# ScalarE's order of block transfers and exponentials in the state-space stages of a hybrid decoder step

## The chip, the cores and the metric

The kernel runs on one core of one Trainium2 chip. A core has five engines that run their own instruction streams and meet at semaphores: PE (TensorE, matmuls and transposes), DVE (VectorE), ACT (ScalarE), POOL (GpSimd) and SP (SyncE, which here only issues transfers). ACT issues transfers too; they stand in its stream between its computations, so a transfer that waits for a semaphore holds back everything behind it on ACT. The metric is the device time of one execution in microseconds (us), lower is better.

## The reference

One step of a two-layer decoder: an attention layer (left as it is here) and a Mamba-2 layer, over a prompt of 16 + 512 tokens and 8 samples of 4 tokens. The part that matters is the state-space part of the Mamba-2 layer:

```python
def ssd_chunked(x, dt, A, B, C, init_state, chunk):
    a_cum = jnp.cumsum(dtg * A.reshape(g, e).astype(f32), axis=2)
    xdt = xg * dtg[..., None]
    seg = a_cum[:, :, :, None] - a_cum[:, :, None, :]
    decay = jnp.exp(jnp.where(causal, seg, -jnp.inf))
    cb = jnp.einsum('bcign,bcjgn->bcijg', Cg, Bg)
    y_diag = jnp.einsum('bcijg,bcijge,bcjgep->bcigep', cb, decay, xdt)
    decay_to_end = jnp.exp(a_cum[:, :, -1:] - a_cum)
    chunk_states = jnp.einsum('bcjgn,bcjge,bcjgep->bcgepn', Bg, decay_to_end, xdt)
    ...
    y_off = jnp.einsum('bcign,bcgepn,bcige->bcigep', Cg, starts, jnp.exp(a_cum))
    y = (y_diag + y_off).reshape(b, L, h, p)
```

`decay` is a 128 x 128 matrix for each head and each chunk, and `exp(a_cum)` a row of 128 for each head and chunk. The states run from chunk to chunk.

## The kernel before

Projections are done in fp32 as three matmuls of a high and a low part (`project`, L1202 to L1204); a weight slab of 1 MB is loaded by SP into one of two buffers, ACT writes its high part (`split_hi`, L689) and POOL the low part (`split_lo`, L608, four instructions). Four attention stages come first, then four state-space stages, one for each group g of 8 heads. PE weaves projections of the stage and the next one between the steps of the state-space part.

A group has six units u: u = 0 is the 32 sample tokens, u = 1 the 16 meta tokens, u = 2 to 5 the four chunks of 128 tokens (called blocks here). The steps of block u, and where they stand:

- `load_a(g, u)` (L985, issued by ACT): the block's cumulative logs are copied out of a scratch in DRAM to all 128 partitions of a tile `seg`, 0.5 MB. There are three such tiles: blocks 2, 3, 4, 5 take tiles 1, 2, 0, 1. Tile 2 lies where the sample states 6 and 7 are held, so `load_a(g, 3)` waits until SP's stores of those two (`out<-s_in`, L564) have landed (`sn_out[6]`, `sn_out[7]`). `load_a(g, 4)` waits for unit 0's matmuls, `load_a(g, 5)` for block 2's (`b_done`).
- POOL subtracts the block's own logs (L660, once the transfer has landed), then ACT clamps and exponentiates the tile (`decays`, L1057 and L1059), then DVE multiplies by the scores (`mix`, L2003).
- `load_ec(g, u)` (L997, ACT, two transfers): the rows for `exp(a_cum)`; blocks 4 and 5 use the two tiles `ec` again, after DVE's `add_skip` of block 2 or 3 (`d_done`). `start_decay(u)` (L1063, ACT) exponentiates them; `add_skip(u)` (L2037 to L2040, DVE) uses them.
- PE: `part_a` (scores and transposes of the block), then `part_b` (L1521 needs `mix`; L1531; L1535 ends with `b_done`).
- POOL's `decay_state` (L621) scales the running state after `b_done`, DVE's `new_state` (L2017) adds to it.

The order on each engine is written out by hand, and no scheduler changes it. PE runs `part_a(u)`, `part_b(u-1)`, one projection, and so on. POOL runs, for blocks 3 to 5, the subtraction of block u, then `decay_state(u-1)`; in the last group POOL splits the last two weight slabs ahead of block 3's subtraction. DVE runs `prepare(u)`, `new_state(u-1)`, `mix(u)`, a projection's evacuation, `add_skip(u-1)`. In the last group the very last slab's high part goes to a tile of its own (`w_hi_last`). At the end of a group ACT squares the gated output (`square_y`, L1122), which PE sums (`sum_y`, L1542).

Of the kernel before, what the change touches and what calls it, by code (L numbers as in the profile page):

```python
# [44 lines left out]
UNITS = len(ORDER)  # L45
# [76 lines left out]
def z_order(stage):  # L122

    if stage == STAGES - 1:
        return [(t, half) for half in range(2) for t in range(4)]
    return [(t, half) for t in range(4) for half in range(2)]
# [37 lines left out]
def build(nc, x_prompt, x_sample, cache_k, cache_v, state_conv, state_ssm, meta_tokens, norm_w,  # L164
# [14 lines left out]
    def slab_done(n):  # L179
        kind, stage, i = slabs[n]  # L180
        return tile_done(kind, stage, per_slab[kind] * (i + 1) - 1)
# [36 lines left out]
    with ctx:  # L218
# [207 lines left out]
        def seg_no(u):  # L426

            return u - 1 if u else 0
# [15 lines left out]
        def high_buf(n):  # L444

            return w_hi_last if n + 1 == len(slabs) else w_hi_buf[n % HI_SLOTS]
# [222 lines left out]
        def _(act):  # L669
# [9 lines left out]
            def split_hi(count=1):  # L679
                for _ in range(count):  # L680
                    n = done[0]
                    m = slab_elems[slabs[n][0]]
                    act.wait_ge(w_raw[n % RAW_SLOTS], raw_target[n])
                    if n + 1 == len(slabs):
                        for b in range(4):
                            act.wait_ge(sn_out[b], 16 * GROUPS)
                    elif n >= HI_SLOTS:
                        act.wait_ge(p_done, slab_done(n - HI_SLOTS))
                    act.activation(high_buf(n)[:, 0:m], raw[n % RAW_SLOTS][:, 0:m],  # L689
                                   ACT.Copy).then_inc(w_hi, 1)  # L690
                    done[0] += 1

            def exp_tables():
                act.preload_act_table_set("natural_log_exp_and_others")
# [276 lines left out]
            def load_a(g, u):  # L971

                c, i = ORDER[u], seg_no(u)
                n = LEN[c]
                if i == 0 and g:
                    act.wait_ge(b_done, UNITS * g)
                if i == 1:
                    act.wait_ge(cn_out, 96 * (g + 1))
                if i == 2:
                    for b in (6, 7):  # L980
                        act.wait_ge(sn_out[b], 16 * (g + 1))
                if i >= 3:
                    act.wait_ge(b_done, UNITS * g + (3 if i == 4 else 1))
                src = a_scratch[SSM_H * g:SSM_H * (g + 1), COL[c]:COL[c] + n]
                act.dma_start(seg[i % SEG_SLOTS][0:n, :, 0:n],  # L985
                              src.partition_broadcast(n)).then_inc(e_in[i % SEG_SLOTS], 16)

            def load_ec(g, u):

                c = ORDER[u]  # L990
                if u >= 4:
                    act.wait_ge(d_done, 5 * g + u - 2)
                elif g:
                    act.wait_ge(d_done, 5 * (g - 1) + u + 2)
                src = a_scratch[SSM_H * g:SSM_H * (g + 1), COL[c]:COL[c] + P].rearrange("(t e) n -> e t n", e=2)
                for i in range(2):
                    act.dma_start(ec[u % 2][64 * i:64 * i + 64, :, :],  # L997
                                  src[i].partition_broadcast(64)).then_inc(ec_in[u % 2], 16)
# [7 lines left out]
            for g in range(GROUPS):  # L1006
# [44 lines left out]
                def decays(u):  # L1051
                    w = 5 * g + seg_no(u)
                    n = LEN[ORDER[u]]
                    act.wait_ge(seg_done, w + 1)
                    e = seg[seg_no(u) % SEG_SLOTS][0:n, :, 0:n]

                    act.activation(e, e, ACT.Relu, scale=-1.0).then_inc(clamped, 1)  # L1057
                    act.wait_ge(clamped, w + 1)
                    act.activation(e, e, ACT.Exp, scale=-1.0).then_inc(l_done, 1)  # L1059

                def start_decay(u):
                    act.wait_ge(ec_in[u % 2], 32 * (2 * g + (u - 2) // 2 + 1))
                    act.activation(ec[u % 2][:, :, :], ec[u % 2][:, :, :], ACT.Exp).then_inc(ec_ready, 1)  # L1063
# [26 lines left out]
                def silu_z(parts):  # L1090
                    for t, half in parts:
                        act.wait_ge(p_evac, half_no[("z", s, t, half)] + 1)
                        act.activation(z[:, t, span("z", s, half)], z[:, t, span("z", s, half)],
                                       ACT.Silu).then_inc(silu_ready, 1)

                for u in range(2, UNITS):
                    decays(u)
                    if u == 2:
                        if g + 1 == GROUPS:
                            split_hi()  # L1100
                        load_a(g, 3)
                        load_a(g, 4)
                    if u == 3:
                        load_a(g, 5)
                        if g + 1 < GROUPS:
                            split_hi()
                    start_decay(u)
                    if 4 <= u + 1 < UNITS:
                        load_ec(g, u + 1)
                    if (g, u) == (GROUPS - 1, 2):  # L1110
                        silu_z(z_order(s)[0:HEADS])
                        exp_tables()
# [556 lines left out]
        def _(dve):  # L1669
# [40 lines left out]
            def soft_max(s, u):  # L1710

                c, v = ORDER[u], UNITS * s + u
                n, cc, b = rows_of(c), colsum(c), v % 2
                dve.wait_ge(s_done, v + 1)
                dve.wait_ge(c_ready, 2 * s + (2 if u else 1))
                if v >= 2:
                    dve.wait_ge(t_done, v - 1)
                if c == 5:
                    dve.tensor_tensor_reduce(sm[b][:, 0:1024], fS, cst[:, C_SATT:C_SATT + 1024], 1.0, 2 * NEG,
                                             ALU.add, ALU.max, mx[:, b, 0:1])  # L1720
                    link(dve.tensor_tensor_reduce(sm[b][:, 1024:1056], misc[:, 32:64],
                                                  cst[:, C_SATT + 1024:C_SATT + 1056], 1.0, 2 * NEG,
                                                  ALU.add, ALU.max, mx[:, b, 1:2]))
                    w = 1
                    link(dve.tensor_tensor(mx[:, b, 0:1], mx[:, b, 0:1], mx[:, b, 1:2], ALU.max))
                    sink = sink_rows[:, s:s + 1]
                else:
                    _, nk, m0 = keys_of(c)
                    for h in range(HEADS):
                        ins = dve.tensor_tensor_reduce(sm[b][0:n, h * 256:h * 256 + nk], fS[0:n, h * 256:h * 256 + nk],  # L1730
                                                       cst[0:n, C_MASK + m0:C_MASK + m0 + nk], 1.0, 2 * NEG,
                                                       ALU.add, ALU.max, mx[0:n, b, h:h + 1])
                    link(ins)
                    w = 4
                    sink = sinks[0:n, 4 * s:4 * s + 4]
                link(dve.tensor_tensor(mxc[0:n, 0:w], mx[0:n, b, 0:w], crow[0:n, cc:cc + w], ALU.mult))
                link(dve.tensor_tensor(msk[0:n, 0:w], mxc[0:n, 0:w], sink, ALU.max))
                dve.tensor_scalar(nm[0:n, b, 0:w], msk[0:n, 0:w], -1.0, None, ALU.mult)
                dve.tensor_tensor(ds[0:n, b, 0:w], sink, msk[0:n, 0:w], ALU.subtract).then_inc(soft_a, 1)
# [487 lines left out]
```

## Time and profile before

| | us |
|---|---|
| median of 3 runs (lowest, highest) | 1024.51 (1024.32, 1026.81) |
| the profiled execution, its own time | 1027.62 |
| span of its trace | 1024.7 |
| PE busy | 980.9 (96%) |
| DVE, ACT, POOL busy | 581.2, 466.9, 365.8 |
| share of PE in the chain that ended last | 79% |

In the rows further down, a timeline row gives the start in the span, the duration, the engine, the line of the kernel, the operation, the tile written and those read, and in square brackets how long the engine had been idle and what ended that. "issue" means that the profile shows no wait that ended there. A waits row gives the waiting instruction, whom it waited for, the sum, how often, and the longest. In a row by stretch the columns are the length, then the busy time of PE, PE's weight loads, DVE, ACT and POOL with their counts, the granted clock of PE, the DMA engines' share and GB/s. Times are us from the start of the span. Group g = 0 of the state-space part has its blocks at 575 to 615, the next two repeat it about 124 and 248 later, and the last (g = 3) has them at 945 to 987.

### The profile page before, as it was taken

How to read it: one execution, taken by the hardware profiler on the slowest of the kernel's cores; microseconds unless marked ns; L12 is line 12 of the kernel's file. 1: busy time of each engine (PE TensorE's matmuls, PEld its weight loads, DVE VectorE, ACT ScalarE, POOL GpSimd, SP SyncE). 2: the span in 40 equal slices, each digit the busy share in tenths (PEclk: the TensorE clock that was granted, in tenths of full speed). 3: DMA queues.
4: the chain of work that ended last, by engine and by line, in shares of the span. 5: the costliest groups of instructions: out<-in, count | busy, mean ns of one | idle time of the engine just before them, and what ended most of it. 6: DMA issues, size and time to landing. Idle time of an engine off the chain costs nothing.

```text
span 1024.7 us, 18539 instructions
## 1 busy us (share of the span) xinstructions
PE 980.9 (96%) x7372; PEld 902.1 (88%) x7372; DVE 581.2 (57%) x1433; ACT 466.9 (46%) x819; POOL 365.8 (36%) x275
## 2 busy tenths in 40 slices
PE   8999999999999999999997999999999999999988
PEld 7988899989998899978986889998799978997867
DVE  5114431354224431356685787966889577986772
ACT  5324623365134623366444364343552445526453
POOL 4240233113330233115533335534354244443610
PEclk9999999999999999999998999999999999999999
DMA  6351221242233222101423715247242563416303
GB/s 198 101 155 62 83 83 53 85 157 65 66 103 141 84 83 59 73 21 42 148 86 87 226 44 157 83 111 205 62 136 84 148 186 82 137 47 207 92 11 98
DMA packets 144117, 106.35 MB, mean 104 GB/s; under 512 B 10258, under 2 KB 135364, under 8 KB 143840
## 3 DMA queue, kind: packets, MB, share of 16 engines
q1 hardware_dynamic: 115032, 92.24, 29.0%
q10 hardware_dynamic: 29000, 12.94, 4.8%
q8 instruction: 58, 0.95, 0.4%
q14 instruction: 27, 0.22, 0.1%
HBM read 92.44 MB, written 16.79 MB: 107 GB/s over the span
## 4 chain that ended last, share of the span: by engine, by line
PE 79%; DVE 10%; issue 4%; DMA 3%; ACT 2%; POOL 2%; ACTq 0%; SPq 0%; DVEq 0%; POOLq 0%
PE pp L1202 19%; PE pp L1204 19%; PE pp L1203 18%; PE pS L1318 3%; DMA w_raw_buf<-in_w_attn_in 2%; PE pS L1542 2%; DVE cv L1914 2%; PE pO L1364 1%; PE pO L1363 1%; PE pO L1535 1%; PE pO L1531 1%; PE pT_ L1521 1%; PE pO L1482 1%; POOL w_lo_raw L608 1%; DVE z L2056 1%
## 5 line engine op out<-in xcount | busy, mean ns | idle before, releaser
L608 POOL TENSOR_TENSOR w_lo_buf<-w_raw_buf,w_hi_buf 128x512 fp32r<-128x512 f32 x214 | 288.0, 1377 | 503.0 <-ACT w_hi_buf L689 272.0
L1202 PE MATMUL pp<-h_hi,w_hi_buf 128*128 128x280 f32 (+1 forms) x1248 | 379.6, 304 | 7.8 <-POOL w_lo_buf L608 2.9
L1204 PE MATMUL pp<-h_hi,w_lo_buf 128*128 128x280 f32 (+1 forms) x1248 | 364.1, 292 | 0.0
L1203 PE MATMUL pp<-h_lo,w_hi_buf 128*128 128x280 f32 (+1 forms) x1248 | 363.5, 291 | 0.0
L1202 PEld LDWEIGHTS pp<-h_hi,w_hi_buf 128*128 128x128 f32 x1248 | 236.7, 190 | 19.0 <-issue 11.7
L1203 PEld LDWEIGHTS pp<-h_lo,w_hi_buf 128*128 128x128 f32 x1248 | 236.4, 189 | 4.6 <-issue 4.1
L1204 PEld LDWEIGHTS pp<-h_hi,w_lo_buf 128*128 128x128 f32 x1248 | 236.4, 189 | 0.0
L689 ACT ACTIVATE w_hi_buf<-w_raw_buf 128x2048 fp32r<-128x2048 f32 (+1 forms) x55 | 104.1, 1892 | 38.7 <-DMA w_raw_buf<-in_w_ssm_in 16.9
L1700 DVE TENSOR_TENSOR x<-x,pp 128x272 f32<-128x272 f32 (+3 forms) x128 | 56.4, 440 | 80.3 <-PE pp L1204 79.4
L1202 PE MATMUL pp<-og_hi,w_hi_buf 128*128 128x280 f32 (+2 forms) x256 | 76.2, 298 | 1.8 <-DVE og_lo L1821 1.1
L1204 PE MATMUL pp<-og_hi,w_lo_buf 128*128 128x280 f32 (+2 forms) x256 | 75.2, 294 | 0.0
L1203 PE MATMUL pp<-og_lo,w_hi_buf 128*128 128x280 f32 (+2 forms) x256 | 75.1, 293 | 0.0
L1914 DVE SCALAR_TENSOR_TENSOR cv<-rb,par,cv 128x584 f32<-128x584 f32 x69 | 69.1, 1001 | 1.1
L1202 PE MATMUL pp<-y_hi,w_hi_buf 128*128 128x272 f32 (+2 forms) x224 | 66.5, 297 | 1.8 <-DVE x L1700 1.5
L1203 PE MATMUL pp<-y_lo,w_hi_buf 128*128 128x272 f32 (+2 forms) x224 | 64.5, 288 | 0.0
L1694 DVE TENSOR_TENSOR q<-pp,rs 128x280 f32<-128x280 f32 x32 | 14.4, 450 | 82.4 <-PE pp L1204 82.4
L1057 ACT ACTIVATE seg<-seg 128x1024 f32<-128x1024 f32 (+1 forms) x20 | 18.6, 932 | 83.5 <-issue 48.4
L1204 PE MATMUL pp<-y_hi,w_lo_buf 128*128 128x272 f32 x192 | 55.4, 289 | 0.0
L1202 PEld LDWEIGHTS pp<-og_hi,w_hi_buf 128*128 128x128 f32 x256 | 48.8, 191 | 2.9 <-issue 2.6
L1773 DVE TENSOR_TENSOR gate<-pp,rs 128x280 f32<-128x280 f32 x32 | 14.4, 449 | 63.8 <-PE pp L1204 63.8
L1203 PEld LDWEIGHTS pp<-og_lo,w_hi_buf 128*128 128x128 f32 x256 | 48.9, 191 | 0.2 <-issue 0.2
L1204 PEld LDWEIGHTS pp<-og_hi,w_lo_buf 128*128 128x128 f32 x256 | 48.8, 191 | 0.0
(334 smaller groups left out, 1730.0 us busy)
## 6 DMA issues: line engine op xcount, KB each, us to landing
w_raw_buf<-in_w_attn_in SPq DMA_DIRECT2D x16, 1024.0 KB, 5.2
w_raw_buf<-in_w_ssm_in SPq DMA_DIRECT2D x16, 1024.0 KB, 5.4
w_raw_buf<-in_w_attn_out SPq DMA_DIRECT2D x8, 1024.0 KB, 5.1
s_in<-in_state_ssm SPq DMA_DIRECT2D x32, 256.0 KB, 4.2
out<-s_in SPq DMA_DIRECT2D x32, 256.0 KB, 3.0
seg<-a_scratch ACTq DMA_DIRECT2D x16, 512.0 KB, 4.1
w_raw_buf<-in_w_ssm_out SPq DMA_DIRECT2D x8, 1024.0 KB, 5.6
w_raw_buf<-in_w_attn_in SPq DMA_DIRECT2D x8, 512.0 KB, 5.9
```

What stands on the lines that cost most here:

```text
L608: ins = pool.tensor_tensor(low_buf(n)[:, piece], raw[n % RAW_SLOTS][:, piece], high_buf(n)[:, piece].bitcast(F32), ALU.subtract)
L689: act.activation(high_buf(n)[:, 0:m], raw[n % RAW_SLOTS][:, 0:m], ACT.Copy).then_inc(w_hi, 1)
L1057: act.activation(e, e, ACT.Relu, scale=-1.0).then_inc(clamped, 1)
L1202: pe.matmul(dst, hi[:, k, cols], a_hi[:, k, tk], start=(k == 0), stop=False)
L1203: pe.matmul(dst, hi[:, k, cols], a_lo[:, k, tk], start=False, stop=False)
L1204: mm = pe.matmul(dst, lo[:, k, cols], a_hi[:, k, tk], start=False, stop=(k == depth - 1))
L1318: mm = pe.matmul(fS[0:n, h * 256:h * 256 + nk], q[:, h, COL[c]:COL[c] + n], kq[:, k0:k0 + nk], start=True, stop=True)
L1542: mm = pe.matmul(pS[:, part, 0:tk.stop - tk.start], ones[:, :], xc[:, t, tk], start=(t == 0), stop=(t == HEADS - 1))
L1694: dve.tensor_tensor(dst[:, tk], bank(kind, s, tile, half), rs[:, tk], ALU.mult).then_inc(p_evac, 1)
L1700: dve.tensor_tensor(x[:, tile, tk], x[:, tile, tk], bank("out", s, tile, half), ALU.add).then_inc(p_evac, 1)
L1773: dve.tensor_tensor(gate[:, t, tk], bank("gate", s, t, half), rs[:, tk], ALU.mult).then_inc(p_evac, 1)
L1914: ins = dve.scalar_tensor_tensor(w[:, 0:CONV_OUT], r[:, tap:tap + CONV_OUT], conv_wc(tap, ct), w[:, 0:CONV_OUT], ALU.mult, ALU.add)
```

## The change

Two moves in ACT's stream, in every group. The transfers of blocks 4 and 3 (in this order now) are issued ahead of block 2's `decays`, where they stood behind it in the other order. And `load_ec` of blocks 4 and 5 is issued behind that block's own `decays`, where it stood one block earlier, behind `start_decay` of the block before. Nothing is added or taken out, and the streams of the other engines are the same.

```diff
                 for u in range(2, UNITS):
+                    if u == 2:
+                        load_a(g, 4)
+                        load_a(g, 3)
                     decays(u)
                     if u == 2:
                         if g + 1 == GROUPS:
                             split_hi()
-                        load_a(g, 3)
-                        load_a(g, 4)
                     if u == 3:
                         load_a(g, 5)
                         if g + 1 < GROUPS:
                             split_hi()
+                    if u >= 4:
+                        load_ec(g, u)
                     start_decay(u)
-                    if 4 <= u + 1 < UNITS:
-                        load_ec(g, u + 1)
```

ACT's stream in group 0, at block 2 (`seg1` is block 2's tile, `seg2` block 3's, `seg0` block 4's; the same in groups 1 and 2):

```order
 L1089 ACTIVATE sT1_138<-pT_ 128x512 [waits yo_done]
-L1057 ACTIVATE seg1_119<-seg1_119 128x1024 [waits seg_done]
-L1059 ACTIVATE seg1_119<-seg1_119 128x1024 [waits clamped]
+L985 DMA seg0_118<-a_scratch 128x8x128 [waits b_done]
 L985 DMA seg2_120<-a_scratch 128x8x128 [waits sn_out7,sn_out6]
-L985 DMA seg0_118<-a_scratch 128x8x128 [waits b_done]
+L1057 ACTIVATE seg1_119<-seg1_119 128x1024 [waits seg_done]
+L1059 ACTIVATE seg1_119<-seg1_119 128x1024 [waits clamped]
 L1063 ACTIVATE ec0_126<-ec0_126 128x512 [waits ec_in0]
```

Both transfers now stand ahead of block 2's two activations, and the activations stand behind a wait for two stores.

ACT's stream in the last group, at the same place (`w_hi_last` is the last weight slab's high part, which POOL's last split reads):

```order
 L1089 ACTIVATE sT1_138<-pT_ 128x512 [waits yo_done]
+L985 DMA seg0_118<-a_scratch 128x8x128 [waits b_done]
+L985 DMA seg2_120<-a_scratch 128x8x128 [waits sn_out7,sn_out6]
 L1057 ACTIVATE seg1_119<-seg1_119 128x1024 [waits seg_done]
 L1059 ACTIVATE seg1_119<-seg1_119 128x1024 [waits clamped]
 L689 ACTIVATE w_hi_last_134<-w_raw0_buf_54 128x2048 [waits sn_out2,sn_out1,sn_out3,sn_out0,w_raw0]
-L985 DMA seg2_120<-a_scratch 128x8x128 [waits sn_out7,sn_out6]
-L985 DMA seg0_118<-a_scratch 128x8x128 [waits b_done]
 L1063 ACTIVATE ec0_126<-ec0_126 128x512 [waits ec_in0]
```

Here the two transfers also pass the last slab's high part.

ACT's stream at block 4, before (`ec0` holds block 4's rows):

```order
L1063 ACTIVATE ec1_127<-ec1_127 128x512 [waits ec_in1]
L997 DMA ec0_126<-a_scratch 64x4x128 [waits d_done]
L997 DMA ec0_126<-a_scratch 64x4x128
L1057 ACTIVATE seg0_118<-seg0_118 128x1024 [waits seg_done]
L1059 ACTIVATE seg0_118<-seg0_118 128x1024 [waits clamped]
L1063 ACTIVATE ec0_126<-ec0_126 128x512 [waits ec_in0]
```

and now:

```order
L1063 ACTIVATE ec1_127<-ec1_127 128x512 [waits ec_in1]
L1057 ACTIVATE seg0_118<-seg0_118 128x1024 [waits seg_done]
L1059 ACTIVATE seg0_118<-seg0_118 128x1024 [waits clamped]
L997 DMA ec0_126<-a_scratch 64x4x128 [waits d_done]
L997 DMA ec0_126<-a_scratch 64x4x128
L1063 ACTIVATE ec0_126<-ec0_126 128x512 [waits ec_in0]
```

Block 4's activations no longer stand behind the wait for DVE's `add_skip`; block 5 is the same with `seg1` and `ec1`.

## Rows read from the trace of the kernel before

**Rows 1.** Page, first line.

```profile
span 1024.7 us, 18539 instructions
```

**Rows 2.** Waits of PE, 570 to 612 (us in total, times, longest).

```profile
PE pT_ L1521 <- issue: 2.1, 3, 1.0
```

**Rows 3.** Waits of PE, 942 to 982.

```profile
PE pS L1542 <- ACT xc L1122: 4.0, 1, 4.0
```

**Rows 4.** Timeline of PE, 570 to 625 (start, duration, instruction, [idle before it]).

```profile
586.90 1.09 PE L1521 MATMUL pT_<-seg,xdt 128*64 128x128 f32 x16 [0.42 <-issue]
...
588.92 1.02 PE L1535 MATMUL pO<-xw,btok 128*128 128x512 f32 x2
...
594.67 1.09 PE L1521 MATMUL pT_<-seg,xdt 128*64 128x128 f32 x16 [0.95 <-issue]
...
602.33 1.09 PE L1521 MATMUL pT_<-seg,xdt 128*64 128x128 f32 x16 [0.77 <-issue]
```

**Rows 5.** Timeline of POOL, 570 to 612.

```profile
588.35 2.27 POOL L660 TENSOR_TENSOR seg<-seg,tok 128x1024 f32<-128x1024 f32 x1 [5.16 <-DMA seg<-a_scratch]
590.59 1.04 POOL L621 TENSOR_TENSOR state<-state,ealast 128x512 f32<-128x512 f32 x1
591.59 1.89 POOL L660 TENSOR_TENSOR seg<-seg,tok 128x1024 f32<-128x1024 f32 x1
...
598.80 2.35 POOL L660 TENSOR_TENSOR seg<-seg,tok 128x1024 f32<-128x1024 f32 x1
```

**Rows 6.** Timeline of DVE, 570 to 612.

```profile
585.58 1.22 DVE L2003 TENSOR_TENSOR seg<-seg,cbm 128x1024 f32<-128x1024 f32 x1
...
592.85 1.72 DVE L2003 TENSOR_TENSOR seg<-seg,cbm 128x1024 f32<-128x1024 f32 x1 [0.43 <-ACT seg L1059]
...
600.66 1.57 DVE L2003 TENSOR_TENSOR seg<-seg,cbm 128x1024 f32<-128x1024 f32 x1 [0.67 <-ACT seg L1059]
```

**Rows 7.** Timeline of ACT, 560 to 610 (ACTq: its queue issues a transfer).

```profile
583.23 1.06 ACT L1057 ACTIVATE seg<-seg 128x1024 f32<-128x1024 f32 x1 [6.92 <-POOL seg L660]
...
584.38 1.02 ACTq L985 DMA_DIRECT2D seg<-a_scratch  x2
```

**Rows 8.** Timeline of SP, 573 to 577.

```profile
575.81 0.92 SPq L564 DMA_DIRECT2D out<-s_in  x2
```

**Rows 9.** Line L564, issued 576.1 to 576.6: issue to landing.

```profile
DMA to landing us min/median/max: 2.2/2.4/2.6
```

**Rows 10.** Line L985, issued 584.3 to 584.8: issue to landing.

```profile
DMA to landing us min/median/max: 3.8/3.8/3.8
```

**Rows 11.** Busy time by stretch: engines, PEclk, DMA share, GB/s last.

```profile
584.00:585.00 1.00, 1.00 (x10) 1.00 (x9) 0.97 (x3) 0.97 (x2) 0.00 (x0) 1.00 1.06 376
```

**Rows 12.** The same, 576.5 to 588.2.

```profile
576.50:588.20 11.70, 11.28 (x93) 9.98 (x91) 9.89 (x18) 2.75 (x3) 6.70 (x5) 1.00 0.96 287
```

**Rows 13.** Timeline of ACT, 928 to 1003.

```profile
945.75 1.05 ACT L1057 ACTIVATE seg<-seg 128x1024 f32<-128x1024 f32 x1
...
947.79 1.90 ACT L689 ACTIVATE w_hi_last<-w_raw_buf 128x2048 fp32r<-128x2048 f32 x1
951.71 1.01 ACTq L985 DMA_DIRECT2D seg<-a_scratch  x2
```

**Rows 14.** Timeline of POOL, 928 to 1003.

```profile
950.09 5.50 POOL L608 TENSOR_TENSOR w_lo_raw<-w_raw_buf,w_hi_last 128x512 fp32r<-128x512 f32 x4
955.63 2.29 POOL L660 TENSOR_TENSOR seg<-seg,tok 128x1024 f32<-128x1024 f32 x1
962.23 1.04 POOL L621 TENSOR_TENSOR state<-state,ealast 128x512 f32<-128x512 f32 x1 [4.31 <-PE pO L1535]
```

**Rows 15.** Timeline of DVE, 928 to 1003.

```profile
956.68 2.32 DVE L2003 TENSOR_TENSOR seg<-seg,cbm 128x1024 f32<-128x1024 f32 x1
```

**Rows 16.** Timeline of PE, 935 to 1025.

```profile
966.31 1.09 PE L1521 MATMUL pT_<-seg,xdt 128*64 128x128 f32 x16 [0.38 <-issue]
```

**Rows 17.** Chain of waits that ended last, 935 to 1025.

```profile
976.91 2.98 DMA ec<-a_scratch
```

## The prediction

> **What bounds the kernel now.** I read first the chain of waits, then who PE waits for in the state-space stages, then the timelines of all engines around those waits. PE is the bound: it fills nearly the whole span of 1024.7 [rows 1], so an edit on ACT is worth only what it takes out of PE's idle time, or adds to it. In group 0 PE waits three times before `part_b`, 2.1 in all [rows 2]: 0.42 before block 2, 0.95 before block 3, 0.77 before block 4 [rows 4]. Groups 1 and 2 repeat this. In the last group PE waits 4.0 for `square_y` [rows 3], and a chain of small steps sets the end there. So the edit can reach three times 2.1, and the last group.
>
> Two of the three waits look like ACT's: `mix` of blocks 3 and 4 started 0.43 and 0.67 after DVE had come free, released by ACT's exponential [rows 6]. But these two `mix` took 1.72 and 1.57, where block 2's took 1.22 [rows 6]. Set them beside POOL [rows 5]. Block 3's `mix` starts at 592.85, while POOL subtracts on block 4 from 591.59 to 593.48, and ends at 594.57, 1.09 behind POOL. Block 4's starts at 600.66, POOL works on block 5 from 598.80 to 601.15, and `mix` ends at 602.23, 1.08 behind POOL. The last group's block 2 is the same: from 956.68 with 2.32 [rows 15], while POOL subtracts from 955.63 to 957.92 [rows 14], ending 1.08 behind it. So a `mix` (two operands in SBUF) does not run beside a POOL subtraction: it stands until POOL's instruction is over. That decides what an earlier ACT is worth.
>
> **The change, part by part.** No instruction is added, so all of it is waits.
>
> (a) `decays` of blocks 4 and 5 no longer stand behind `d_done`. ACT then has block 4's exponentials ready as soon as POOL has subtracted. The gain is nothing: `mix(4)` follows `new_state(3)`, which waits for POOL's `decay_state(3)`, and POOL starts block 5's subtraction right behind that; `mix(4)` ends 1.08 behind it whether ACT is early or not. PE's 0.77 stays. `load_ec` keeps its own wait for `d_done`, and `start_decay` sat behind the landing already: in the last group the chain runs from the issue at 976.91 through 2.98 of transfer [rows 17], with no exponential on it. Cost 0, gain 0, bounds 0 to -0.77 per group.
>
> (b) The two block transfers move ahead of block 2's `decays`; queued behind `load_a(3)`'s wait are those `decays` and, in the last group, the last slab's `split_hi`. In groups 0 to 2 this wait is covered: ACT was idle for 6.92 until POOL's subtraction let `decays(2)` start at 583.23 [rows 7]. SP issued the two stores at 575.81 and about 576.3 [rows 8], the later landed 2.6 after its issue [rows 9], at 578.9. With 0.5 MB of `load_a(4)` now beside them I add up to 1.8 (its bytes at the 287 GB/s of [rows 12]), 580.7 at the latest. Still before 583.2, so it costs ACT nothing, with 2.5 of cover.
>
> What it gains: POOL waited 5.16 for block 3's transfer, subtracted from 588.35 to 590.62 [rows 5], and so began `decay_state(2)` at 590.59, though block 2's `b_done` came at 589.94 [rows 4]. With the transfer early, `decay_state(2)` starts at about 590.0, block 4's subtraction ends 0.55 earlier, and so does `mix(3)`, which hangs on that by the overlap above, not on ACT. PE's wait before block 3 falls from 0.95 to about 0.40. The last group shows that state already: there POOL was free, idle for 4.31 before `decay_state(2)` [rows 14], and PE waited 0.38 [rows 16]. Gain 0.55 a group, 1.65 in three.
>
> What it can lose: block 3's subtraction now falls early, and may fall onto `mix(2)`, which runs from 585.58 to 586.80 [rows 6] and for which PE already waits 0.42. Where does the transfer land? From the first store to the end of `load_a(3)`, 0.5 + 0.5 + 1.0 + 0.5 = 2.6 MB must pass (stores, `load_a(4)`, a weight slab, `load_a(3)`). At the best stretch's 376 GB/s [rows 11] that takes 7.0, at the mean of 287 [rows 12] 9.1. From about 576.5 (first store issued at 575.81, [rows 8]) it ends at 583.5 to 585.6. A transfer of 0.5 MB landed 3.8 after its issue [rows 10], of which its bytes are 1.5; I count 1.0 of the other 2.3 as behind the last byte. Landing: 584.5 to 586.6, and later if the next slab's load, which SP issues as soon as POOL has split the slab before, takes a share. `mix(2)` starts at 585.58. If the load lands behind that, `mix(2)` runs first, POOL subtracts from 586.8 to 588.7 while DVE has slack, and nothing is lost. I take this as the likelier half.
>
> (c) The last group. Here ACT was not idle. Before, it ran `decays(2)` at 945.75 and `split_hi` at 947.79, and then stood until 951.71 for the stores [rows 13]. Now it stands first: `load_a(3)` still goes out at 951.7, `decays(2)` runs from 952.1 to 954.2, `split_hi` until 956.1. `mix(2)` does not notice (it began at 956.68, [rows 15]). POOL does: its split of the last slab started at 950.09 and took 5.50 [rows 14], and now starts at 956.2, 6.1 later. Block 3's subtraction and `decay_state(2)` stand behind it, with 4.31 of slack [rows 14]. The excess is 6.1 - 4.31 = 1.8; 1.4 if the subtraction takes the 1.89 of [rows 5] instead of 2.29. If `load_a(4)` holds up the stores, up to 1.8 more: 3.6. I take 1.8. It goes from `decay_state(2)` through block 4's subtraction and `mix(3)` into PE, `d_done`, `load_ec(5)`, `square_y` and the end, with nothing on the way to absorb it.
>
> Sum: -1.65 + 1.8 = about +0.1 on the span of 1024.7. The profiled execution took 1027.62 by its own clock, 3 more than its span; the runs' median of 1024.51 lies at the span. I apply the difference to the median: 1024.6.
>
> **The rivals.**
> - *Collision, slower.* The transfer lands before 585.5, POOL takes block 3's subtraction ahead of `mix(2)`, and PE's wait before block 2 grows by 1.1 (as in [rows 15], 2.32 against 1.22) to 1.9 (the whole subtraction); I take 1.5. Against the 0.55 gained, each group loses 0.95, three lose 2.85, and with the last group's 1.8 it is +4.65: 1029.2. For it speaks the byte sum at the best rate, against it the next slab. It decides at a landing of 585.5 and, with one or two groups hit, lies between. The Trainium skill, "DMA: Bandwidth & Descriptors", section "Queues, rings and completion order", says that each DMA engine takes its queue rows in turn, packet by packet. By that `load_a(3)` would get its turns beside SP's weight slabs, which makes this rival likelier; no row here shows a small load in the middle of a slab.
> - *ACT was the limit, faster.* If `mix(3)` and `mix(4)` do not have to wait for POOL, all of 0.95 + 0.77 = 1.72 goes in three groups, -5.2, and with the last group's +1.8 it is 1021.1. For it speaks that the profile puts the release of both on ACT, against it the three ends at 1.08 to 1.09 behind POOL.
> - *It does not come earlier.* ACT's transfers are held up behind the slabs and block 3 lands at 588 as before. Then only (c) is left: 1026.3.
>
> **How the numbers follow.** Forecast 0.50, collision 0.28, ACT as the limit 0.12, no earlier landing 0.10. A measurement of this kernel can tell about 0.3%, 3.1 here, from no change. Forecast and late landing lie inside that but for the end of (c), about 0.04. The collision passes it in three cases of four, 0.20. ACT as the limit passes it in two of three, 0.08. So 0.08 faster, 0.68 same, 0.24 slower. The range takes in the forecast with (c) from 1.4 to 3.6, the collision up to 1.3 a group, and most of the faster rival: 1021.2 to 1030.2; the forecast alone spans 1024.2 to 1026.5.
>
> **What would show it.** In groups 0 to 2: POOL's L660 on block 3 without the 5.16 wait; `decay_state(2)` 0.1 behind L1535 of block 2; PE's wait before block 3 at 0.4, before block 4 still near 0.8 though ACT finishes long before `mix(4)`; PE's wait before block 2 at 0.42 (forecast) or 1.5 and more (collision, with L2003 of block 2 at 2.3). In the last group: L689 on `w_hi_last` at 954 instead of 947.8, POOL's last L608 from 956, PE's wait before block 3 at 2 instead of 0.38. I am wrong if PE's wait before block 4 falls, if the last group does not stretch, or if a PE wait appears that is not named here.

## The result

The changed kernel takes 1034.05 us (median of 4 runs, 1032.07 to 1034.97), the kernel before 1024.84 in the same comparison: a ratio of 1.0088 with a 95% interval of 1.0073 to 1.0103. The prediction said 1024.6, at most 1030.2. It is slower by 9.2, and 4 above the end of the range.

In the changed kernel's listing the lines behind the edit carry a number one higher: `part_b`'s first product, the one that needs `mix`, is L1522, its last L1536, `mix` is L2004, `sum_y` L1543. The lines of ACT, POOL and SP that matter keep theirs. The page's first line of the changed kernel:

```profile
span 1032.2 us, 18539 instructions
```

The two traces are 7.5 apart (1024.7 in [rows 1]), a little less than the 9.2 of the medians.

The timeline of PE in the state-space stages of the changed kernel, the rows with an idle time before them (start, duration, instruction, [idle before it]); they answer to [rows 4], [rows 16] and [rows 3]:

```profile
585.91 1.09 PE L1522 MATMUL pT_<-seg,xdt 128*64 128x128 f32 x16 [0.40 <-issue]
594.68 1.93 PE L1522 MATMUL pT_<-seg,xdt 128*64 128x128 f32 x16 [1.94 <-issue]
603.49 1.09 PE L1522 MATMUL pT_<-seg,xdt 128*64 128x128 f32 x16 [0.33 <-issue]
...
719.49 1.09 PE L1522 MATMUL pT_<-seg,xdt 128*64 128x128 f32 x16 [0.37 <-issue]
727.14 1.09 PE L1522 MATMUL pT_<-seg,xdt 128*64 128x128 f32 x16 [0.77 <-issue]
...
845.52 1.09 PE L1522 MATMUL pT_<-seg,xdt 128*64 128x128 f32 x16 [2.33 <-issue]
...
971.42 1.97 PE L1522 MATMUL pT_<-seg,xdt 128*64 128x128 f32 x16 [5.02 <-issue]
...
988.20 2.05 PE L1543 MATMUL pS<-xc,ones 128*128 128x256 f32 x4 [3.88 <-ACT xc L1123]
```

Group 1 did what was forecast: 0.37 before block 3 instead of 0.93, 0.77 before block 4 as ever. That was luck, as a run with the same two transfers early shows further down (1.77 there). Groups 0 and 2 wait 1.94 and 2.33 before block 3, where 0.40 was expected, and the last group 5.02 where 2 was. Behind the first and the last of these waits the 16 matmuls take 1.93 and 1.97 instead of 1.09.

Who is late? The timeline of ACT in the changed kernel, groups 0 and 2 (ACTq: its queue issues a transfer):

```profile
574.77 6.18 ACTq L985 DMA_DIRECT2D seg<-a_scratch  x2
582.24 1.06 ACT L1057 ACTIVATE seg<-seg 128x1024 f32<-128x1024 f32 x1 [6.91 <-POOL seg L660]
...
824.42 0.45 ACTq L985 DMA_DIRECT2D seg<-a_scratch  x1
832.46 0.37 ACTq L985 DMA_DIRECT2D seg<-a_scratch  x1
832.87 1.06 ACT L1057 ACTIVATE seg<-seg 128x1024 f32<-128x1024 f32 x1 [7.89 <-DMA out<-s_in]
```

The answer to [rows 9], line L564 with the stores of states 6 and 7 of group 0, issue to landing in the changed kernel, minimum, median and maximum:

```profile
DMA to landing us min/median/max: 2.9/4.1/5.3
```

And the answer to [rows 10], line L985, `load_a(3)` of group 0, issued at 580.6:

```profile
DMA to landing us min/median/max: 8.0/8.0/8.0
```

`load_a(4)` goes out at 574.77, just ahead of the two stores (574.83 and 575.24). The trace's records of packets show what that does: the first store's 512 packets pass until 577.3, from there to 578.5 only `load_a(4)`'s do, and the later store's 512 pass from 578.5 to 580.1. So that store lands 5.3 after its issue (2.6 before), `load_a(3)` can go out only at 580.6, and then takes 8.0 (3.8 before): it lands at 588.6, no earlier than in the kernel before. In group 2 the store is later still, `load_a(3)` goes out only at 832.46, and there ACT itself was held: `decays(2)` waited 7.89 for the store, not for POOL.

The timeline of POOL in the changed kernel, group 0 and the last group (it answers to [rows 5] and [rows 14]):

```profile
588.74 1.90 POOL L660 TENSOR_TENSOR seg<-seg,tok 128x1024 f32<-128x1024 f32 x1 [6.53 <-DMA seg<-a_scratch]
...
960.08 5.45 POOL L608 TENSOR_TENSOR w_lo_raw<-w_raw_buf,w_hi_last 128x512 fp32r<-128x512 f32 x4 [6.95 <-ACT w_hi_last L689]
965.49 1.89 POOL L660 TENSOR_TENSOR seg<-seg,tok 128x1024 f32<-128x1024 f32 x1
967.35 1.04 POOL L621 TENSOR_TENSOR state<-state,ealast 128x512 f32<-128x512 f32 x1
```

And ACT in its last group, which answers to [rows 13]:

```profile
948.34 7.66 ACTq L985 DMA_DIRECT2D seg<-a_scratch  x2
...
956.05 1.06 ACT L1057 ACTIVATE seg<-seg 128x1024 f32<-128x1024 f32 x1 [7.67 <-DMA out<-s_in]
...
958.11 1.90 ACT L689 ACTIVATE w_hi_last<-w_raw_buf 128x2048 fp32r<-128x2048 f32 x1
```

The last group is the chain that the prediction described, only longer: `decays(2)` at 956.05 (952.1 foretold), `split_hi` from 958.11, POOL's last split at 960.08 (956.2 foretold), `decay_state(2)` at 967.35 instead of 962.23. Of these shifts 1.8 was there before the edit acts in this group: its last store went out at 949.0, not 947.2.

Following the start of `part_b` (L1521, now L1522) through both traces, changed minus before: block 2 of group 0 -0.99 (it was there before the first changed instruction), block 3 of group 0 +0.01, block 4 of group 0 +1.16, block 4 of group 1 +0.60, block 4 of group 2 +2.65, and in the last group block 2 +0.45, block 3 +5.11, block 4 +7.3, `sum_y` +7.2. Of the 2.2 that the last group gives back ahead of its block 2, 0.7 is a shorter wait of PE for DVE (0.40 instead of 1.10 before L1451, now L1452) and about 1.4 is the clock: from 945 to 950 PE's granted clock was 0.67 in the kernel before, that is, partly at its lower level (1.2 GHz), and 1.00 in the changed kernel.

### The profile page after: what moved, and what is told of

The parts are those of the page before. It is cut to its first block, busy times and chain, and to the rows that moved or that the text cites. A ratio compares the mean times of both kernels' runs of the same rounds, so it can differ in the third digit from the quotient of the medians.

```text
span 1032.2 us, 18539 instructions
## 1 busy us (share of the span) xinstructions
PE 984.3 (95%) x7372; PEld 905.4 (88%) x7372; DVE 581.9 (56%) x1433; ACT 466.2 (45%) x819; POOL 364.0 (35%) x275
## 4 chain that ended last, share of the span: by engine, by line
PE 77%; DVE 11%; issue 5%; DMA 3%; POOL 2%; ACT 2%; ACTq 0%; SPq 0%; DVEq 0%; POOLq 0%
PE pp L1203 19%; PE pp L1205 18%; PE pp L1204 18%; PE pS L1319 3%; DVE cv L1915 2%; DMA w_raw_buf<-in_w_attn_in 2%; PE pS L1543 2%; PE pT_ L1522 2%; PE pO L1532 1%; PE pO L1536 1%; PE pO L1365 1%; PE pO L1364 1%; PE pO L1483 1%; DVE z L2057 1%; POOL w_lo_raw L608 1%
```

## The experiments

The theory was: `load_a(4)`, half a megabyte on ACT's queue, runs in the way of SP's stores 6 and 7; `load_a(3)`, and all that ACT has queued behind its wait, hang on these stores. The rivals: the later decay rows cost something; the wait's new place is enough by itself; one place (the last group) carries it all.

**One half each.** The kernel before, with `load_ec` moved alone:

```diff
+                    if u >= 4:
+                        load_ec(g, u)
                     start_decay(u)
-                    if 4 <= u + 1 < UNITS:
-                        load_ec(g, u + 1)
```

> The kernel before with one half of the change: the decay rows of the last two units are issued behind their own block's exponentials; the block transfers stay where they were. Theory (the stores of states 6 and 7, delayed by load_a(4) beside them, carry the loss): this half is worth nothing, 1024.5 within 1.0, PE's wait before block 4 stays at 0.77 in groups 0 to 2, since mix(4) ends behind POOL's subtraction whether ACT is early or not. Rival 1 (the later issue of the decay rows carries a part of the loss, in the last group, where the chain runs through them): 2 us or more above before. Rival 2 (ACT was the limit before block 4): 2 to 3 below before.

Measured: 1023.94 against 1024.16, ratio 0.9998 (0.9989 to 1.0007). PE's timeline, block 4 of group 0:

```profile
599.60 1.09 PE L1521 MATMUL pT_<-seg,xdt 128*64 128x128 f32 x16 [0.77 <-issue]
```

Nothing, and 0.77 stays, as step (a) had it. The other half, the two transfers alone:

> The kernel before with the other half: load_a(4) and load_a(3) ahead of block 2's decays, the decay rows as before. Theory (stores delayed by load_a(4)): the whole loss, 1032 to 1035, with the stores of states 6 and 7 landing 5 or more after their issue in group 0 (2.6 before) and PE waiting 4 to 5 before block 3 in the last group. Rival (the loss needs both halves, or lies in the decay rows): 1024 to 1028.

Measured: 1032.82, ratio 1.0076 (1.0058 to 1.0094), PE's wait before block 3 of the last group 5.05; the later store of group 0 landed 5.0 after its issue. The whole loss is in the transfers. Before block 3 of groups 0, 1 and 2 PE waits 1.43, 1.77 and 3.15 here: group 1, which gained in the changed kernel's profile (0.37), loses with the same transfers.

**The order of the two transfers.** The changed kernel, but:

```diff
                     if u == 2:
-                        load_a(g, 4)
                         load_a(g, 3)
+                        load_a(g, 4)
```

> The changed kernel with the two early transfers in the other order: load_a(3), which waits for the stores, then load_a(4). So nothing of ACT's runs beside the stores. Theory (load_a(4) in the stores' way is the cause): the stores of group 0 land 2.6 after their issue again, load_a(3) goes out at about 579, decays(2) starts with POOL's subtraction, PE's wait before block 3 falls to 0.4 in groups 0 to 2; in the last group only the wait of the prediction's step (c) is left, 1.8 to 3.6. Sum 1024.5 to 1027. Rival (the place of load_a(3)'s wait ahead of block 2's exponentials is enough, whoever runs beside the stores): 1031 to 1035, with the last group's wait of about 5 before block 3 unchanged.

Measured: 1029.52, ratio 1.0044 (1.0029 to 1.0059): half of the loss is gone, and half is not. The sum was missed. The later store lands 2.6 after its issue again (in group 1 it took 4.1, though nothing of ACT's was beside it) and `load_a(3)` goes out at 577.7, three earlier than in the changed kernel. But look at PE, group 0:

```profile
587.03 1.09 PE L1522 MATMUL pT_<-seg,xdt 128*64 128x128 f32 x16 [1.78 <-issue]
594.24 1.09 PE L1522 MATMUL pT_<-seg,xdt 128*64 128x128 f32 x16 [0.37 <-issue]
```

at POOL and at DVE of the same kernel, block 3's subtraction and block 2's `mix`:

```profile
583.95 1.90 POOL L660 TENSOR_TENSOR seg<-seg,tok 128x1024 f32<-128x1024 f32 x1 [2.00 <-DMA seg<-a_scratch]
```

```profile
584.34 2.59 DVE L2004 TENSOR_TENSOR seg<-seg,cbm 128x1024 f32<-128x1024 f32 x1
```

This is the prediction's collision rival: `mix(2)` begins 0.39 behind POOL's subtraction, ends at 586.93, 1.08 after it, and takes 2.59 instead of 1.22. PE waits 1.78, 1.51 and 1.55 before block 2 in groups 0, 1 and 2, 1.1 to 1.4 more than the 0.42 of before (the rival's price was 1.1 to 1.9), and gets 0.37 to 0.39 before block 3. `load_a(3)` took 6.1 to land even so. In the last group PE still waits 3.95 before block 3. Block 2's `part_b` ended there at 960.85 (L1536, 959.83 and 1.02), and `decay_state(2)` started 3.65 later:

```profile
964.50 1.04 POOL L621 TENSOR_TENSOR state<-state,ealast 128x512 f32<-128x512 f32 x1
```

So with the stores undisturbed, step (c) alone is 3.6 in this execution, twice what was taken for it. The sum is not the same in every run: two of the eight took 1025.0 and 1025.5, the other six 1029.0 to 1030.7.

**Where the loss lies.** The change in groups 0 to 2 alone:

> The changed kernel in groups 0 to 2; in the last group the block transfers stand where they stood before. Theory (two thirds of the loss come in the last group, where ACT holds POOL's last split and PE's clock falls behind the wait): the shift of 2.5 at the start of the last group's stages stays, the last group is as before: 1026.5 to 1028. Rival 1 (the last group carries all): 1024.5. Rival 2 (the last group merely passes on what comes late from the others): 1032 to 1034.

Measured: 1027.66 (1024.68 to 1032.79), ratio 1.0036 (1.0021 to 1.0051): +3.5. PE's waits before block 3 are 1.35, 0.37 and 2.30 in its profile (and 1.41 before block 2 of group 2), and 0.39 in the last group. The profiled execution is the fastest of the ten, so its waits show the place of the loss and not all of it. Its runs spread over 8, the kernel before's over 5: what lands when is not the same in every run. And in the last group alone:

> The kernel before in groups 0 to 2; in the last group load_a(4) and load_a(3) stand ahead of block 2's decays as in the change. Theory (the change's parts add up: groups 0 to 2 alone were 3.5 above the kernel before, the whole change 9.3): this is 5 to 6.5 above before, 1029.5 to 1031, with ACT waiting some 7 for the stores, POOL's last split 8 to 10 after the old time, and PE waiting 4.5 to 5.5 before block 3 with the granted clock at its lower level behind that wait. Rival (the last group's wait comes from what groups 0 to 2 shifted, its stores meeting load_a(4) only then): 1 to 3 above before.

Measured: 1029.0, ratio 1.0049 (1.0034 to 1.0064): +4.8, a little less than expected. ACT and PE of its last group:

```profile
951.63 1.06 ACT L1057 ACTIVATE seg<-seg 128x1024 f32<-128x1024 f32 x1 [8.15 <-DMA out<-s_in]
```

```profile
967.02 1.09 PE L1524 MATMUL pT_<-seg,xdt 128*64 128x128 f32 x16 [4.09 <-issue]
```

3.5 and 4.8 make 8.3; the two transfers together cost 8.7. The parts add up within their intervals.

**`load_a(4)` alone early,** `load_a(3)` with its wait at the old place:

```diff
                     if u == 2:
                         load_a(g, 4)
-                        load_a(g, 3)
                     decays(u)
                     ...
+                        load_a(g, 3)
```

> The changed kernel with load_a(4) alone ahead of block 2's decays; load_a(3), which waits for the stores, stands behind them as before. So the stores are disturbed, and ACT does not wait for them ahead of its exponentials. Theory (the loss comes through what stands behind the wait for the stores): the stores of group 0 still land about 5 after their issue, but ACT's decays(2) start with POOL's subtraction, POOL's last split starts at its old time, and PE's wait before block 3 in the last group is below 1: 1023.5 to 1025.5. Rival (the early bytes of load_a(4) do the harm by themselves, by holding up slabs or load_a(3)): 1028 or more.

Measured: 1028.28, ratio 1.0038 (1.0024 to 1.0052). The theory was right on the last group (0.38 before block 3) and wrong on the others; the sum is the rival's. PE of groups 0 and 2, block 3:

```profile
594.50 1.09 PE L1522 MATMUL pT_<-seg,xdt 128*64 128x128 f32 x16 [2.29 <-issue]
...
844.89 1.09 PE L1522 MATMUL pT_<-seg,xdt 128*64 128x128 f32 x16 [3.05 <-issue]
```

`load_a(3)` went out at its old place, behind `decays(2)` (582.85; all of this group is 1.5 earlier here), and was late: POOL's subtraction on block 3 started at 588.56 after 6.89 of waiting. The transfer took 5.6 to land (3.8 before), and the weight slabs, which stand behind the stores on SP's queue, were late too: they landed 7.2 and 8.9 after their issue, 5.4 and 6.9 in the kernel before. So the early bytes cost something without any wait of ACT's.

**The slabs.** The order with `load_a(3)` first, and SP's next slabs held until it has landed:

```diff
+                sp.wait_ge(*seg_landed(g, 3))
                 load_slabs(min(slab_no[("z", s, 1)] + 4, len(slabs)))
```

> The kernel with load_a(3) ahead of load_a(4), both early in all groups, and SP's next weight slabs held until load_a(3) has landed. In that order without the hold load_a(3) landed 6.2 after its issue in group 0, beside a slab that SP had issued 2.1 before it. Theory (a block transfer that is issued while a slab is in flight is held up by it): load_a(3) lands 3 to 4 after its issue in groups 0 to 2, POOL subtracts on block 3 right behind block 2 and is done before mix(2) starts, so mix(2) takes 1.2 again and PE waits 0.4 before block 2 and 0.4 before block 3. The last group (no slabs there) keeps its wait of 4 before block 3. Sum 1025 to 1027. Rival (the 0.5 MB of load_a(4) behind it, or the rows themselves, make load_a(3) slow): it lands 5 to 7 after its issue as before, mix(2) still takes over 2.2 and PE waits 1.5 before block 2. Rival on the other side (the slabs, some 5 later, are late for the splits of ACT and POOL): 1029 and more, with a new wait of PE in the projections.

Measured: 1027.19, ratio 1.0021 (1.0009 to 1.0033). Line L986 here (`load_a`), `load_a(3)` of group 0:

```profile
DMA to landing us min/median/max: 3.5/3.5/3.5
```

Without a slab in flight the transfer lands after 3.5, not 6.1 or 8.0. POOL subtracts on block 3 right behind block 2, and `mix(2)` takes 1.21. PE's wait before block 2 is 0.75 and not the expected 0.4, before block 3 it is 0.37. (Both slabs are held here, so the share of the second one alone is not tested.) DVE of group 0 shows why:

```profile
582.40 1.27 DVE L1995 TENSOR_TENSOR xw<-xdt,wend 128x512 f32<-128x512 f32 x1
...
584.20 1.21 DVE L2005 TENSOR_TENSOR seg<-seg,cbm 128x1024 f32<-128x1024 f32 x1
```

POOL's second subtraction, from 581.18 to 583.1, now lies on `xw`, which takes 1.27 instead of 0.69. The overlap has only moved to another instruction of DVE. What is left of the loss is the last group, where PE waits 2.70 before block 3, less than the 4 that was expected; the section on the prediction comes back to that.

**The last group's order.** The kernel before, with both transfers early in the last group, and the last slab's `split_hi` ahead of them:

```diff
+                    if (g, u) == (GROUPS - 1, 2):
+                        split_hi()
+                        load_a(g, 3)
+                        load_a(g, 4)
                     decays(u)
```

> The kernel before in groups 0 to 2. In the last group both transfers stand ahead of block 2's decays, as in the change (load_a(3) first), but the last slab's split_hi stands ahead of them. Theory (in the last group the loss runs over POOL, whose last split waits for split_hi): POOL's last split starts at or before its old time, decays(2) end at about 954 to 955, ahead of when mix(2) began before, and PE's wait before block 3 is below 0.8: 1023.5 to 1025.5. Rival (the held exponentials of block 2 are what counts): PE waits 1.5 or more before block 2, 1026 or more.

Measured: 1024.32, ratio 0.9995 (0.9984 to 1.0006). ACT and POOL in the last group:

```profile
943.88 1.90 ACT L689 ACTIVATE w_hi_last<-w_raw_buf 128x2048 fp32r<-128x2048 f32 x1
949.47 1.01 ACTq L985 DMA_DIRECT2D seg<-a_scratch  x2
```

```profile
948.72 3.76 POOL L608 TENSOR_TENSOR w_lo_raw<-w_raw_buf,w_hi_last 128x512 fp32r<-128x512 f32 x3
```

`split_hi` done, POOL splits at its time, and holding `decays(2)` until 950.53 costs nothing in the sum. PE's 0.79 before block 2 is not the hold's: `mix(2)` did not wait for ACT, and the kernel with `load_ec` alone moved has 0.69 there. In the last group the loss ran over POOL's last split, not over block 2's exponentials.

**The overlap itself.** The kernel before, with one wait added on POOL:

```diff
                         pool.wait_ge(*seg_landed(g, u))
+                        if u >= 3:
+                            pool.wait_ge(m_done, 5 * g + seg_no(u - 1) + 1)
```

> The kernel before, with the transfers where they were, and one wait added: POOL's subtraction of a block starts when DVE's mix of the block before it is done. Theory (a mix stands while POOL subtracts, and this, not ACT, makes PE wait before blocks 3 and 4): every mix takes 1.2; mix(3) is then held by ACT's exponentials, which end at 592.85 in group 0, so PE's wait before block 3 falls from 0.95 to about 0.45; mix(4) comes about 1.1 earlier, and PE's wait of 0.77 before block 4 goes to 0.3 or less. 1.0 to 1.3 a group in all four groups: 1019.5 to 1021.5. Rival (ACT or the length of mix for another reason sets these waits): 1023.5 to 1025, the waits before block 4 still at 0.77. Rival on the other side (the later subtraction holds ACT's exponentials, which then come too late): over 1025, PE's wait before block 4 over 1.

Measured: 1019.74 against 1024.9, ratio 0.9946 (0.9931 to 0.9962). `mix` on DVE and the waits of PE, blocks 3 and 4 of group 0:

```profile
591.80 1.23 DVE L2005 TENSOR_TENSOR seg<-seg,cbm 128x1024 f32<-128x1024 f32 x1 [0.42 <-ACT seg L1061]
599.16 1.23 DVE L2005 TENSOR_TENSOR seg<-seg,cbm 128x1024 f32<-128x1024 f32 x1 [0.72 <-ACT seg L1061]
```

```profile
593.12 1.09 PE L1523 MATMUL pT_<-seg,xdt 128*64 128x128 f32 x16 [0.45 <-issue]
600.49 1.09 PE L1523 MATMUL pT_<-seg,xdt 128*64 128x128 f32 x16 [0.48 <-issue]
```

All 16 `mix` of the blocks take 1.21 to 1.23, and 0.95 and 0.77 become 0.45 and 0.48 (0.3 or less was expected for the second). It was POOL that set these waits; only now is it ACT, with 0.42 and 0.72 ahead of `mix`. A wait that was added makes the kernel 0.5% faster.

**The change's idea with both costs taken away.** That wait, the decay rows as in the change, and in groups 0 to 2 the transfers early, `load_a(3)` first; the last group as before:

> The added wait of POOL's subtraction behind the mix of the block before, and in groups 0 to 2 both transfers early in the order that leaves the stores alone: load_a(3), then load_a(4). The last group's transfers stand as before. Theory (the early transfer's gain in groups 0 to 2 was given back as a collision of block 3's subtraction with mix(2)): PE waits about 0.4 before each of blocks 2 and 3 and 0.3 or less before block 4 in groups 0 to 2: 0.5 a group below the kernel with the added wait alone, 1018.5 to 1020.5. Rival (the early transfer is held up behind the weight slabs in some group and gives nothing): 1020 to 1022. Rival (the collision is not what made PE's wait before block 2 grow): that wait stays at 1.5 and more, 1023 and up.

Measured: 1017.33, ratio 0.9927 (0.9912 to 0.9943), a little better than expected and the fastest kernel here, 0.7% below before and 1.6% below the changed one. POOL and PE of group 0:

```profile
586.82 1.90 POOL L662 TENSOR_TENSOR seg<-seg,tok 128x1024 f32<-128x1024 f32 x1 [3.78 <-DVE seg L2007]
```

```profile
586.75 1.09 PE L1525 MATMUL pT_<-seg,xdt 128*64 128x128 f32 x16 [0.40 <-issue]
593.50 1.09 PE L1525 MATMUL pT_<-seg,xdt 128*64 128x128 f32 x16
600.32 1.09 PE L1525 MATMUL pT_<-seg,xdt 128*64 128x128 f32 x16
```

Block 3's transfer has landed long before POOL may use it, and PE waits 0.40 before block 2, while before blocks 3 and 4 the rows show no wait. All pieces early in all four groups, the last slab's `split_hi` first:

> All pieces that helped or cost nothing: load_a(3), then load_a(4), early in all four groups, the last slab's split_hi ahead of them in the last group, the decay rows behind their block's exponentials, and POOL's subtraction behind the mix of the block before. Theory: as the kernel with the early transfers in groups 0 to 2 and the added wait (1017.3), the last group neither better nor worse: 1016 to 1018.5. Rival (without the last group's old place its transfers meet the stores there): 1019 or more.

Measured: 1017.54, ratio 0.9930 (0.9915 to 0.9946), the same. Last, the changed kernel word for word, with only the added wait:

> The changed kernel, word for word, with POOL's subtraction behind the mix of the block before. Theory (the change's loss comes over the stores and the late block 3, not over the collision of subtraction and mix): the waits before block 3 of 1.9 in group 0, 2.3 in group 2 and 5.0 in the last group stay within 0.6, only the waits before block 4 shrink: 1029.5 to 1033, 12 or more above the same kernel with load_a(3) first. Rival (the collision carries the loss): below 1024.

Measured: 1029.79, ratio 1.0046 (1.0030 to 1.0062), 12.3 above the kernel with all pieces, which has the better order and also the last `split_hi` first; the better order alone with this wait was not run. PE's waits before block 3 in groups 2 and 3 stay:

```profile
842.21 1.37 PE L1524 MATMUL pT_<-seg,xdt 128*64 128x128 f32 x16 [2.38 <-issue]
...
967.97 1.98 PE L1524 MATMUL pT_<-seg,xdt 128*64 128x128 f32 x16 [4.54 <-issue]
```

The added wait takes 4.3 off the changed kernel and took 5.2 off the kernel before, so the loss does not lie in the overlap of `mix` and subtraction. Block 3 came too late in the changed kernel to collide with `mix(2)`, which took 1.22 or 1.23 in all four groups.

## Why the prediction was wrong, by its own steps

- **(a), the decay rows: right.** Worth nothing by themselves, 0.77 before block 4 stays, and `mix` ends 1.08 behind POOL. The wait added on POOL shows the cause, which the prediction had only argued. The Trainium skill, "SBUF — State Buffer", section "SBUF: two separate sides", gives the rule: a VectorE operation with two SBUF inputs and a GpSimd operation that reads SBUF exclude each other, and the one that starts second stands. The trace agrees, with 1.22 alone and 2.59 behind POOL.
- **(b), the gain: right where it could come.** 0.93 to 0.37 in group 1 of the changed kernel (by luck, see above), and 0.37 to 0.39 in all three groups once the stores were left alone.
- **(b), the transfer's landing: the step that failed in groups 0 and 2, some 3.5 of the 9.2.** It counted 2.6 MB ahead of and with `load_a(3)`, with one slab, and left the second slab to a half-sentence ("later if the next slab's load ... takes a share"). Two passed: the late stores let `load_a(3)` go out only at 580.58, and SP had issued the second slab just ahead of it, at 580.42. With 1.0 more (the prediction's 0.5 is 524288 bytes) the 2.6 MB are 3.7, and at the 287 GB/s of [rows 12] they take 12.8. The first store was issued at 574.83, 1.0 earlier than before, so the count starts at 575.5 and ends at 588.3; the load landed at 588.6. The price was in the rows; the second slab was not in the sum. The kernel with both slabs held shows what slabs cost, 3.5 to land instead of 6.1.
- **(b), the cover of ACT's wait: thin, and broken in one group.** The stores were to land at 580.7 at the latest and did so at 580.5 in group 0, though with 5.3 after the issue and not the bound's 4.4. In group 2 it was 7.5, and the cover of 2.5 was gone: `decays(2)` began on the store.
- **(c), the last group: right in its chain, its 1.8 too small by 3.0.** Alone it costs 4.8: PE's wait before block 3 grew from 0.38 to 4.09, 3.7, and behind it PE's granted clock was 0.65 from 967 to 971 (next point). Two terms were mis-sized. First the stores: with `load_a(4)` in their way the later one lands 6.6 after its issue in the changed kernel's last group (6.7 in the kernel with the last group alone), 4.5 in the kernel before: 2.1, where at most 1.8 was allowed for and none was taken. Then the slack of 4.31 [rows 14], which is that of one execution: in it the later store was issued at 947.2 and block 2's `part_b` ended at 962.15, 15.0 later, PE having run a part of this at its lower clock. In the kernel with `load_a(3)` first it was 13.2 (947.6 to 960.85) with a clock of 1.00 from 945 to 950, in the changed kernel 13.6. Whatever is missing from the 15.0 goes straight into the excess: with the stores landing in 4.4, and 13.2, it is 3.65 and not 1.8. The kernel with the slabs held, whose last group is the same, is the other case: 14.8 with a clock of 0.66 from 944 to 949, the store landing in 3.7, and `decay_state(2)` 2.40 late. So with undisturbed stores 1.8 was near in one execution and half of the price in another.
- **What was not named: PE's clock behind the new wait.** In the changed kernel's last group the stretch from the start of block 3's `part_b`, and the same work in the kernel before (time, engines, PEclk, DMA share, GB/s):

```profile
971.40:977.00 5.60, 5.58 (x27) 4.24 (x28) 3.94 (x8) 1.02 (x1) 0.00 (x0) 0.50 0.21 52
```

```profile
966.30:969.30 3.00, 2.99 (x27) 2.35 (x28) 2.93 (x7) 0.00 (x0) 0.00 (x0) 1.00 0.00 0
```

The same work took 3.0 at 1.00, so about 2.6 came on top of the wait itself. In group 0 too: block 3's `part_b` started where it did before (594.68 and 594.67), and with a clock of 0.57 from 594.5 to 598.5 block 4's came 1.16 later. In the kernel before the stretch from 945 to 950 was the slow one, as its own row shows, in the changed kernel not (1.00), and this gave about 1.4 back:

```profile
945.00:950.00 5.00, 3.90 (x36) 3.36 (x33) 3.40 (x10) 4.49 (x5) 4.83 (x4) 0.67 0.64 187
```

- **The rivals.** "ACT was the limit" falls with the added wait. "It does not come earlier" is what happened in groups 0 and 2, by the slabs that it named. "Collision" did not happen in the changed kernel, and did, at the lower end of its price and with its `mix` of over 2.3, as soon as the transfer came early: it was the next obstacle, not the first.

## What to carry to other kernels

A transfer that waits for another's landing pays for everything that any queue issues in between: count all the bytes that will be in flight until it lands, above all those that were issued before it, the next weight slab too, and look at what your own early transfer does to the stores that you wait for. Before moving a wait up on an engine, list what stands behind it there; one instruction that another engine needs (here `split_hi`) belongs ahead of it. And where two instructions on DVE and POOL read SBUF at the same time, ask who should go first: one added wait was worth 0.5%, or 5.2, more than the 1.65 that the prediction gave the early transfers.

## What the runs showed of the hardware

How two queues share the transfers can be counted from the trace's records of packets. In group 0 of the changed kernel the first slab is issued at 575.85, the second at 580.42 and `load_a(3)` at 580.58. ACT's packets (512 bytes) against the slabs' on SP's queue (1024 bytes), by microsecond:

```
from   SP's queue   ACT's queue
581       357            0
582       341            1
583       240           99
584       248          234
585       242          241
586       111          358
```

For over 2 us the first slab ran alone; then the second slab and `load_a(3)` had the same number of packets, which is half the bytes for the smaller ones. The Trainium skill, "DMA: Bandwidth & Descriptors", section "Queues, rings and completion order", says that an engine takes its queue rows in turn, packet by packet. From 584 on the trace agrees (248 and 234, 242 and 241).

In the kernel with `load_a(3)` first the trace shows no such turns. The first slab is issued at 575.58, `load_a(3)` and `load_a(4)` at 577.68 and 578.11, the second slab at 580.17:

```
from   SP's queue   ACT's queue
579       350            0
580       142          345
581        16          612
582         0          676
583       168          336
584       318           48
```

The first slab's 1024 packets end within 581, with the last 16. ACT's two transfers then run almost alone, and the second slab gets its first packets at 583.2, 3.0 after its issue. In the stretches counted here, transfers passed in the order in which the two queues had issued them, and only two issued 0.16 apart took turns. So `load_a(3)` paid for the slabs that were issued ahead of it: its first packets came 2.5 after its issue here, 2.4 in the changed kernel, and 1.1 with the slabs held. Why the order of issue counts over two queues, no run shows.

The clock did not follow the length of the wait. In the changed kernel, behind 1.94 in group 0 and 5.02 in the last group the 16 matmuls took 1.93 and 1.97, behind 2.33 in group 2 of the same run 1.09, and the granted clock stayed at 1.00 there until 857. With the change in the last group alone the 16 matmuls behind 4.09 took 1.09, and only the eight behind them took 1.96 instead of 1.16. What decides that stays open.
